# Experts' results of a mixture-of-experts layer scattered to rows of (choice, token)

## The reference, cut to what matters

```python
scores = sigmoid(xs @ router_w); sel = scores + router_bias
# the best 4 of 8 groups of experts, then the 6 best experts in them
_, idx = top_k(where(emask, sel, -inf), TOP_K)
w = scores[idx] / sum(scores[idx]) * ROUTED_SCALE
yg = (silu(xg @ w1[e]) * (xg @ w3[e])) @ w2[e]     # for each (token, expert) pair
routed = segment_sum(yg * w, token)                # 6 results per token are added
out = routed + swiglu(xs, sh_w1, sh_w3, sh_w2)     # the shared expert
```

## Time and profile before

| | us |
|---|---|
| median of the three runs (2195.92 to 2200.32) | 2196.2 |
| the profiled execution | 2184.72 |
| its span, first to last instruction | 2182.9 |
| TensorE busy | 1844.7 |
| VectorE busy | 872.6 |
| ACT busy | 468.2 |
| POOL busy | 366.8 |
| expert loop of layer 0, about | 530 to 1130 |
| expert loop of layer 1, about | 1490 to 2092 |

### The profile page before, as it was taken

One profiled execution on the slowest core, in us unless ns is written; L12 is line 12 of the kernel. 1 busy time (PEld: TensorE's weight loads), 2 busy tenths in 40 slices (PEclk: granted clock), 3 DMA queues, 4 the chain that ended last, 5 costly groups with the idle time before them and its releaser, 6 DMA issues.

```text
span 2182.9 us, 30725 instructions
## 1 busy us (share of the span) xinstructions
PE 1844.7 (85%) x9320; PEld 956.6 (44%) x9321; DVE 872.6 (40%) x1533; ACT 468.2 (21%) x833; POOL 366.8 (17%) x559
## 2 busy tenths in 40 slices
PE   5989999888999888888981898879988799988952
PEld 3455555334544444444440443344544445444521
DVE  1456656555322222222126499574322222221225
ACT  4134444221111110111110564321111111110102
POOL 0010000001011111111104388001111111111122
PEclk9999999999999999999995999889999999999985
DMA  9487011256899999999988102364999999999954
GB/s 393 175 348 307 1 39 56 114 205 265 302 414 393 407 399 396 397 401 393 390 311 307 78 1 115 114 246 172 368 409 400 397 394 411 395 400 397 389 182 174
DMA packets 94960, 625.09 MB, mean 286 GB/s; under 512 B 16048, under 2 KB 16176, under 8 KB 56880
## 3 DMA queue, kind: packets, MB, share of 16 engines
q1 hardware_dynamic: 43920, 499.70, 57.2%
q0 software_dynamic: 26112, 79.72, 10.0%
q10 hardware_dynamic: 24864, 44.84, 5.7%
HBM read 563.38 MB, written 76.28 MB: 293 GB/s over the span
## 4 chain that ended last, share of the span: by engine, by line
PE 51%; DMA 22%; DVE 10%; POOL 4%; issue 4%; ACT 3%; DVEq 0%; ACTq 0%; SPq 0%; POOLq 0%
DMA ring<-in 20%; PE PS L1024 10%; PE PS L1030 9%; PE PS L1051 5%; PE PS L1037 5%; PE PS L1062 3%; PE PS L1253 3%; PE PS L953 3%; PE PS L1015 3%; POOL work L598 2%; PE PS L1006 2%; POOL work L571 2%; PE PS L971 2%; PE PS L981 2%; DMA y_rows<-work 2%
## 5 line engine op out<-in xcount | busy, mean ns | idle before, releaser
L1030 PE MATMUL PS<-ring,work 128*64 128x256 f32 x3360 | 417.3, 405 | 109.8 <-issue 107.1
L1030 PEld LDWEIGHTS PS<-ring,work 128*64 128x64 f32 x3360 | 248.3, 145 | 254.5 <-issue 159.6
L1417 DVE TENSOR_TENSOR work<-work,PS 64x256 f32<-64x256 f32 x105 | 44.4, 423 | 523.6 <-ACT work L654 520.0
L1037 PE MATMUL PS<-ring,work 128*64 128x512 f32 x840 | 204.8, 609 | 3.0 <-ACT work L680 2.5
L1024 PE MATMUL PS<-ring,work 128*128 128x512 f32 x368 | 164.8, 601 | 13.9 <-issue 8.0
L523 POOL COPY col_i<-idx 128x1 int32 (+1 forms) x128 | 23.2, 181 | 839.8 <-PE PS L1062 825.1
L1422 DVE COPY work<-PS 128x1024 f32<-128x1024 f32 x128 | 156.7, 1225 | 12.5 <-PE PS L1062 2.2
L529 POOL DMA_INDIRECT work<-h_rows,col_i x128 | 124.8, 975 | 167.5 <-issue 167.5
L654 ACT ACTIVATE work<-PS 64x256 f32<-64x256 f32 x105 | 39.4, 375 | 482.5 <-PE PS L1030 480.2
L1062 PE MATMUL PS<-cst,work 128*128 128x128 f32 x1040 | 141.0, 279 | 0.0
L1062 PEld LDWEIGHTS PS<-cst,work 128*128 128x128 f32 x1040 | 113.6, 142 | 54.2 <-issue 54.2
(11 more groups left out here) (238 smaller groups left out, 2171.5 us busy)
## 6 DMA issues: line engine op xcount, KB each, us to landing
ring<-in SPq DMA_DIRECT2D x154, 2048.0 KB, 17.4
ring<-in SPq DMA_DIRECT2D x128, 1024.0 KB, 18.0
y_rows<-sq POOLq DMA_DIRECT2D x2, 14336.0 KB, 57.9
y_rows<-work ACTq DMA_DIRECT2D x210, 128.0 KB, 8.9
ring<-in SPq DMA_DIRECT2D x3, 4096.0 KB, 14.0
ring<-in SPq DMA_DIRECT2D x4, 3072.0 KB, 11.9
y_rows<-work ACTq DMA_DIRECT2D x46, 256.0 KB, 10.2
h_rows<-work ACTq DMA_DIRECT2D x8, 512.0 KB, 15.3
```

What stands on the lines that cost most here:

```text
L1030: last = mm(bank(6)[64 * q:64 * q + 64, 0:F], lhs(c)[:, 0:64], w13(s)[:, q, c, :], start=(c == 0), stop=(c == DC - 1), tile_position=(0, 6 ...
L1037: last = mm(bank(4)[64 * q:64 * q + 64, :], actT[par][:, kk, 0:64], w2(s)[:, kk, q * 512:(q + 1) * 512], start=(kk == 0), stop=(kk == 1), ...
```

## The change

Each expert's result rows are written by an indirect DMA from POOL to the row choice * 512 + token of `y_rows`, which now has 3072 rows. The list of these places, `place_i`, comes from the same products as before, with `tok_hi` and `unit_hi` now holding 128 * (choice * 4 + tile); the token list `idx` is its low bits. In the loop POOL issues the gather of expert u+4 and then, after waiting for the copy into `yb`, the scatter of expert u (`scatter`). `store` on ACT keeps only the copy, for a small expert as two copies of 64 partitions x 512, since a scatter moves whole rows. Past the end of the list the index fails the bounds check. `extra_gather` holds the lines of the old loop over extra blocks, and its scatter comes after the last four of the main loop. The combination is issued from ACT as 24 plain DMAs of 128 rows that follow one another in DRAM; `row_i`, its arithmetic and the zero fill are gone.

```diff
-    y_rows = nc.dram_tensor("y_rows", (ROWS, D), f32, kind="Internal").ap()
+    y_rows = nc.dram_tensor("y_rows", (K * T, D), f32, kind="Internal").ap()
...
+                def scatter(u, n, w):
+                    pool.wait_ge(m["y_ev"], w + 1)
+                    nc.gpsimd.tensor_copy(dst_i[:, n:n + 1], place_i[:, ds(u, 1)]).then_inc(dst_rdy, 1)
+                    pool.wait_ge(dst_rdy, u + 1 + i * E)
+                    nc.gpsimd.tensor_tensor(tick[0:1, 8 * i + 5:8 * i + 6], zero[0:1, 0:1], zero[0:1, 0:1], ALU.add)
+                    big = nc.gpsimd.value_load(big_i[0:1, ds(u, 1)], min_val=0, max_val=1)
+
+                    def rows(p):
+                        pool.indirect_dma_start(out=y_rows, out_offset=bass.IndirectOffsetOnAxis(ap=dst_i[0:p, n:n + 1], axis=0),
+                                                in_=yb[n][0:p], in_offset=None, bounds_check=K * T - 1, oob_is_err=False).then_inc(y_out[n], 16)
+
+                    with nc.gpsimd.If(big > 0):
+                        rows(128)
+                    with nc.gpsimd.Else():
+                        rows(64)
+
                 gather(0, 0, xg_in[0])
                 gather(1, 1, xg_in[1])
-                with nc.gpsimd.Fori(0, E // 2 - 1) as g:
+                for u in range(2, 6):
+                    pool.wait_ge(xgT_ps, u - 1 + i * E)
+                    gather(u, u % 2, xg_in[u % 2])
+                    if u >= 4:
+                        scatter(u - 4, u % 2, place(u - 4))
+                with nc.gpsimd.Fori(0, E // 2 - 3) as g:
                     for r in range(2):
-                        pool.wait_ge(xgT_ps, g * 2 + (1 + r) + i * E)
-                        gather(g * 2 + (2 + r), r, xg_in[r])
+                        pool.wait_ge(xgT_ps, g * 2 + (5 + r) + i * E)
+                        gather(g * 2 + (6 + r), r, xg_in[r])
+                        scatter(g * 2 + (2 + r), r, g * 2 + place(2 + r))
...
+                def extra_scatter(j):
+                    pool.wait_ge(m["t_yev"], j + 2)
+                    nc.gpsimd.tensor_tensor(tick[0:1, 8 * i + 4:8 * i + 5], zero[0:1, 0:1], zero[0:1, 0:1], ALU.add)
+                    nc.gpsimd.tensor_copy(dst_i[:, 0:1], place_i[:, ds(j + E, 1)]).then_inc(m["t_dst"], 1)
+                    pool.wait_ge(m["t_dst"], j + 1)
+                    nc.gpsimd.tensor_tensor(tick[0:1, 8 * i + 7:8 * i + 8], zero[0:1, 0:1], zero[0:1, 0:1], ALU.add)
+                    pool.indirect_dma_start(out=y_rows, out_offset=bass.IndirectOffsetOnAxis(ap=dst_i[:, 0:1], axis=0),
+                                            in_=yb[0], in_offset=None, bounds_check=K * T - 1, oob_is_err=False).then_inc(m["t_yout"], 16)
+
                 with nc.gpsimd.If(many > 0):
-                    with nc.gpsimd.Fori(0, many) as j:
-                        pool.wait_ge(m["t_xgT_ps"], j + 1)
-                        nc.gpsimd.tensor_tensor(tick[0:1, 8 * i + 3:8 * i + 4], zero[0:1, 0:1], zero[0:1, 0:1], ALU.add)
-                        nc.gpsimd.tensor_copy(col_i[:, 0:1], idx[:, ds(j + E, 1)]).then_inc(m["t_idx"], 1)
-                        pool.wait_ge(m["t_idx"], j + 1)
-                        nc.gpsimd.tensor_tensor(tick[0:1, 8 * i + 6:8 * i + 7], zero[0:1, 0:1], zero[0:1, 0:1], ALU.add)
-                        pool.indirect_dma_start(out=xg[0], out_offset=None, in_=h_rows[i],
-                                                in_offset=bass.IndirectOffsetOnAxis(ap=col_i[:, 0:1], axis=0),
-                                                bounds_check=T - 1, oob_is_err=False).then_inc(m["t_xg"], 16)
-
-                pool.wait_ge(zero_out, 32)
-                for s in range(2):
-                    pool.wait_ge(y_out[s], 32 * E // 2 + i * 16 * E)
-                pool.wait_ge(m["dn_ps"], TT + E)
+                    extra_gather(0)
+                for u in range(E - 4, E):
+                    scatter(u, u % 2, place(u))
                 with nc.gpsimd.If(many > 0):
-                    pool.wait_ge(m["t_yout"], many * 16)
-                    nc.gpsimd.tensor_tensor(tick[0:1, 8 * i + 4:8 * i + 5], zero[0:1, 0:1], zero[0:1, 0:1], ALU.add)
-                pool.wait_ge(rows_rdy, i + 1)
-                for n in range(TT * K):
-                    t, q = n // K, n % K
-                    if n >= 6:
-                        pool.wait_ge(comb_used, n - 5 + i * TT * K)
-                    pool.indirect_dma_start(out=comb[n % 6], out_offset=None, in_=y_rows,
-                                            in_offset=bass.IndirectOffsetOnAxis(ap=row_i[:, q * TT + t:q * TT + t + 1], axis=0))\
-                        .then_inc(comb_in[n % 6], 16)
...
-            pool.wait_ge(lat_rdy, 8)
-            for n in range(2):
-                nc.gpsimd.memset(sq[:, n], 0.0).then_inc(zero_rdy, 1)
-            pool.wait_ge(zero_rdy, 2)
-            zeros = sq[:, :, :].rearrange("p a t -> p (a t)").unsqueeze(1).to_broadcast([128, E // 4 + XMAX // 2, D])
-            for n in range(2):
-                pool.dma_start(y_rows[64 * E:ROWS, :].rearrange("(a p u) d -> p a u d", p=128, a=2)[:, n], zeros).then_inc(zero_out, 16)
...
                     if not (isinstance(wait_n, int) and wait_n == 0):
-                        a.wait_ge(y_out[par], wait_n + i * 16 * E)
+                        a.wait_ge(y_out[par], wait_n + i * 8 * E)
                     if big:
                         A(yb[par], bank(4, 2), ACT.Copy).then_inc(m["y_ev"], 1)
                     else:
-                        A(yb[par][:, 0:512], bank(4), ACT.Copy).then_inc(m["y_ev"], 1)
-                    a.wait_ge(m["y_ev"], n + 1)
-                    p = 128 if big else 64
-                    rows = y_rows[0:p * E, :].rearrange("(p e) d -> p e d", e=E)
-                    for half in range(2):
-                        src = yb[par][:, half * 512:(half + 1) * 512] if big else yb[par][64 * half:64 * half + 64, 0:512]
-                        a.dma_start(rows[:, ds(u, 1), half * 512:(half + 1) * 512].rearrange("p e d -> p (e d)"), src)\
-                         .then_inc(y_out[par], 16)
+                        A(yb[par][0:64, 0:512], bank(4)[0:64], ACT.Copy)
+                        A(yb[par][0:64, 512:D], bank(4)[64:128], ACT.Copy).then_inc(m["y_ev"], 1)
...
                         A(yb[0], bank(4, 2), ACT.Copy).then_inc(m["t_yev"], 1)
-                        a.wait_ge(m["t_yev"], j + 2)
-                        a.dma_start(y_rows[128 * E:ROWS, :].rearrange("(u p) d -> p u d", p=128)[:, ds(j, 1), :]
-                                    .rearrange("p u d -> p (u d)"), yb[0]).then_inc(m["t_yout"], 16)
                         a.wait_ge(m["t_yout"], j * 16 + 16)
                         A(tick[0:1, i:i + 1], zero[0:1, 0:1], ACT.Copy).then_inc(tail_end, 1)
+                for n in range(2):
+                    a.wait_ge(y_out[n], 8 * E * (i + 1))
+                for n in range(TT * K):
+                    t, q = n // K, n % K
+                    if n >= 6:
+                        a.wait_ge(comb_used, n - 5 + i * TT * K)
+                    a.dma_start(comb[n % 6], y_rows[q * T + t * 128:q * T + (t + 1) * 128, :]).then_inc(comb_in[n % 6], 16)
...
                 V.tensor_scalar(k4(tok_lo), hot[:, :, 0:TT], k("next"), None, ALU.mult)
-                for t in range(1, TT):
-                    last = V.tensor_scalar(k4(tok_hi)[:, :, t], hot[:, :, t], 128.0 * t, None, ALU.mult)
+                V.tensor_tensor(k4(tok_hi), hot[:, :, 0:TT], k("step").rearrange("p (k t) -> p k t", k=K).unsqueeze(3).to_broadcast([128, K, TT, E]),
+                                ALU.mult)
...
-                link(V.tensor_scalar(score_gap, bank(7)[:, 384:384 + E], 0.5, float(NONE), ALU.is_lt, ALU.mult))
-                V.scalar_tensor_tensor(idx[:, 0:E], bank(7)[:, 384:384 + E], -1.0, score_gap, ALU.add, ALU.add).then_inc(idx_rdy, 1)
+                link(V.tensor_scalar(score_gap, bank(7)[:, 384:384 + E], 0.5, float(NONE + 1), ALU.is_lt, ALU.mult))
+                link(V.scalar_tensor_tensor(place_i[:, 0:E], bank(7)[:, 384:384 + E], -1.0, score_gap, ALU.add, ALU.add))
+                V.tensor_scalar(idx[:, 0:E], place_i[:, 0:E], NONE + T - 1, None, ALU.bitwise_and).then_inc(idx_rdy, 1)
...
-                    V.scalar_tensor_tensor(main_k.rearrange("p (k t) -> p k t", k=K), pos_k.rearrange("p (k t) -> p k t", k=K), float(E),
-                                           topi.rearrange("p (t k) -> p k t", k=8)[:, 0:K], ALU.mult, ALU.add)
-                    link(V.scalar_tensor_tensor(row_k, unit_k, 128.0, at_k, ALU.mult, ALU.add))
-                    link(V.scalar_tensor_tensor(row_k, row_k, 128.0 * (E - 1), main_k, ALU.add, ALU.subtract))
-                    V.tensor_scalar(blk_k, blk_k, 0.5, None, ALU.is_gt)
                     link(V.scalar_tensor_tensor(unit_k, unit_k, -1.0, off_k, ALU.add, ALU.add))
-                    link(V.tensor_tensor(row_k, row_k, blk_k, ALU.mult))
-                    V.tensor_tensor(row_i[:, :], row_k, main_k, ALU.add).then_inc(rows_rdy, 1)
...
```

(3 more changed lines are left out.)

48 lines of the change are left out of this document (31 added, 17 removed).

## The result

The kernel after took 2203.6 us in the median (2201.3 to 2210.3, 18 runs), the kernel before in the same sessions 2193.4 (2188.4 to 2205.7, 18 runs). The ratio is 1.0048, with a 95% interval of 1.0037 to 1.0060: **slower by 10 us**, where 28 us less were forecast. The profiled execution of after has a span of 2205.1 us. That pair of profiles differs by 22 us, twice what the medians do, so shares and rates are read from them, and differences of the end from the medians.

A forecast was written before the change was run, and what follows sets the result against it. The prediction took DMA traffic in the expert loops as the bound. Loops -23, combination -6 and small edits +1 gave -28 us, from 2196.2 to 2168.2 us, range 2150 to 2194.

The forecast's parts named there:

- What bounds the kernel: Expert loops: DMA traffic, mainly expert weights, paces small experts; any byte removed saves its DMA time while TensorE has waiting left.
- Part 1: Expert loops: scatter replacing whole-row stores frees 30.8 us of DMA time, of which 23 us reach the end.
- the small edits: Row and index arithmetic: one product for three, an added mask instruction, more narrow matmuls; 0 to +1 us, +1 taken.
- price of the scatter: Expert loops: a scatter costs the gather's own queue share, 6.3% in layer 0, against the old store's 9.1%.
- The factor 0.75: Expert loops: share of freed DMA time reaching the end, since big experts, about a quarter of the loops, give nothing back.
- Part 2: Scatter on POOL's queue: POOL has room, landing takes 8.8 us, and the result buffer comes free in time.
- Rival B: Expert loops: ACT's copy waits for the scatter from two experts earlier, holding TensorE; +55 us, 2251 us, chance 0.06.
- Part 3: Combination: 24 plain reads from ACT run back to back in 33.0 us; 3 us gained per layer, start unchanged.
- Part 4: Small edits outside the loops cost 0 to +1 us, +1 taken; removing the zero fill gains nothing, at most 4.3 us.
- Rival A: Expert loops: valid rows in low partitions load always the same engines, so the loops gain nothing; 2194 us, chance 0.15.
- Rival D: Loops and tail: random writes cost as much as old ones, tail 2 us later per layer; 2183 us, chance 0.12.

The follow-up runs named there:

- a_midg: Kernel after with only its small experts' 64-row gathers moved to partitions 32 to 95: 2151.0 us, 0.9802 of before.
- b_mid: Kernel before with its small experts' 64-row gathers moved to partitions 32 to 95: 2159.7 us, 0.9851 of before.
- a_mids: Kernel after with only its small experts' scatters reading partitions 32 to 95, gathers left low, four ACT copies: 2226.0 us, 1.0142 of before.
- a_twoscatters: Kernel after with every expert's rows scattered a second time, into an array nobody reads: 2284.1 us, 1.0417 of before.
- a_both128: Kernel after with 128 indices in gather and scatter of every expert, rows packed at low partitions: 2252.3 us, 1.0264 of before.
- a_deal64: Kernel after, small transfers still 64 indices on partitions 0 to 63, places dealt out over groups of four partitions: 2213.9 us, 1.0082 of before.
- a_even: Kernel after with 128 indices in gather and scatter and rows dealt out over groups of four partitions: 2139.2 us, 0.9734 of before.
- b_gather128: Kernel before with every gather over 128 indices, the same rows moved: 2201.9 us, 1.0025 of before.

## Why the prediction was wrong, step by step

**What bounds the kernel**: right that the weights' transfers do. Over all versions the weights' MB in the window and the time moved together (157.7 MB at 2328 us to 183.1 MB at 2128 us), and moving rows to other partitions brought the end forward by up to 62 us. Wrong was what was drawn from it, that any byte taken from the loops is worth its DMA time.

**Part 1** is the step that failed: -23 us were forecast. Measured is the total of +10; with the combination's measured -5 and the +1 that was put down for the small edits taken out, the loops lost about 14 us. (In the pair of profiles, which is 12 us further apart, the time from an expert loop's first gather to its last grew by 18 and 8 us.) Not the term "price of the scatter" was wrong: q0 has 11.5 and 12.2% for the forecast's doubled 12.6 and 12.8. Wrong was what the sum left out, that the weights would go on at 39.6 engine-us per MB beside it. I took all that isn't q10 as fixed, and the weights rose to 41.4, which alone eats the 3.9 points that the other queues gave back. The trace of before held a sign of it: 39.6 is more than the 309 ns x 1 MB / 8192 bytes = 37.7 of an undisturbed packet, and the prediction doesn't use it.

One cause is shown: the gathers' writes to partitions 0 to 63 (a_midg, b_mid, against a_mids). With them moved the change is worth -0.5% in place of +0.5%, about 22 of the 38 us between forecast and result, give or take 8. Whether it is the ports, or fewer engines for these partitions, isn't shown. The rest is open, and so is why low gathers hurt more beside scatters than beside plain stores (41.4 and 39.6, where a_midg and b_mid have 39.2 and 38.5). Neither where the scatters read (a_mids) nor how many there are (a_twoscatters) decides it.

The factor 0.75 was no help either. The second store and the second scatter cost what their share says or more, and with the gathers on 32 to 95 the change is worth at best 0.5%, 11 us, of which some 5 are the combination's, and with the scatters moved too and packed rows it is a loss of 0.5%. Even in the three pairs where it is no loss, the saved 3.1 to 3.6 points of share go in good part to weights that cost 1 to 2% more and to a sum of shares that is 1.1 to 1.7 points lower.

**Part 2**, no wait: right. ACT waits less than before, 17.6 us in 5 cases, and scatters land in 8.9 us where 8.8 was taken. Rival B, that the scatter becomes the wait, is out for this kernel; a_both128 shows it in the other form, with 513 us.

**Part 3**: right in kind, a size off. 2.0 and 3.2 us for the 3 a layer that were forecast, since the adds of layer 0 take 33.7 us and not 33.0; the first add of layer 1 comes 7.2 us after the last copy, as worked out.

**Part 4**: right for the zero fill (70.73 and 70.72 us of TensorE). The small edits weren't tested apart.

**Rival A** gave 2194, with 0.15 of the chance, and came nearest. One of its signs came true, the sum of shares fell by 1.6 points, but dealing out didn't bring it back (98.8% in a_deal64), so that it fell for uneven engines isn't shown. I argued against it that the share was 1.01 with uneven gathers already there. That share counts lengthened packets too, so it couldn't show that the engines did only useful work. The rule of the Trainium skill that stood behind this rival ("DMA: Bandwidth & Descriptors", The descriptor swizzle) is one for transfers to 128 partitions, and there the runs agree with it: 2252 us packed (a_both128), 2139 dealt out (a_even). **Rival D** took half of part 1 away and still gave 2183; the loss came out beyond it. No rival had a mechanism by which the transfers that stay become dearer, and so the range ended at 2194, 10 us short, and slower had 0.07.

## What to carry to other kernels

Where DMA is the bound, read for each queue engine-time per MB and not only its share: a transfer that takes few bytes away can make the bytes of the others dearer, and a full DMA share hides it. Before taking bytes away, look where the small indirect transfers lie: half-height tiles on partitions 32 to 95 in place of 0 to 63 gained 1.5 and 2.5% here for two changed slices, more than the change under study gained in any form. Move the tiles that DMAs write; the tiles that scatters read were better left low, as long as their rows were packed. Then deal the valid rows out over the groups of four partitions: that gained 0.5 to 1.9% with the gathers on 32 to 95, and nothing on 0 to 63.

## What the runs showed of the hardware

- A gather over 64 indices with rows of 4 KB, written to partitions 0 to 63, lengthens weight packets that are under way to all partitions: of the 8 KB ones 31% are over 340 ns in after and 13% in before, and 3% in both with the gather on 32 to 95. This agrees with the port map of the Trainium skill ("SBUF — State Buffer", Door 1: The DMA port swizzle). The same page ("Can I just issue two DMAs to hit both halves?") says that only a transfer that spans all 128 partitions reaches all ports; the measurement is against it as far as packets show: a_midg and b_mid, with 64 partitions on 32 to 95, have 8 KB packets as short as b_gather128 with 128 (317 and 315 ns, for 317).
- Reading is not the mirror of writing: moving the scatters' source to 32 to 95 cost 0.6 to 1.0% with packed rows. With rows dealt out it cost nothing (0.9716 for 0.9749, with intervals that overlap).
- Full height is no cure by itself: 128 indices with packed rows left the shares at 96.1% of the window and the 16 KB packets at 671 ns in the mean, and dealing the same rows out raised the rate from 369 to 409 GB/s.
